# Sixty-four gate groups on the matrix engine: one fp32 product a token in place of three bfloat16 parts

## The reference

```python
def block(hb):
    q = (hb @ w_pq).reshape(TOK_BLOCK, PEER_HEADS, 2, PEER_DHALF)
    s = jnp.einsum('thpd,hpnd->thpn', q, sub_keys)
    s1, i1 = lax.top_k(s[:, :, 0], PEER_TOPK)          # first key, 16 of 128
    s2, i2 = lax.top_k(s[:, :, 1], PEER_TOPK)          # second key, 16 of 128
    cand_s = s1[..., :, None] + s2[..., None, :]
    cand_i = i1[..., :, None] * N_KEYS + i2[..., None, :]
    top_s, pos = lax.top_k(cand_s.reshape(..., 256), PEER_TOPK)
    idx = take_along_axis(cand_i, pos)                 # 16 experts a head, 8 heads
    gate = softmax(top_s)
    act = gelu(einsum('thkd,td->thk', expert_u[idx], hb))
    return einsum('thk,thkd->td', gate * act, expert_v[idx])
```

## Time and profile before

| | |
|---|---|
| median of three runs | 1565.65 us |
| profiled execution | 1565.16 us, span 1563.0 us |
| TensorE busy | 1477.0 us (94%) |
| VectorE busy | 1063.6 us (68%) |
| ScalarE busy | 724.0 us (46%) |
| GpSimd busy | 306.3 us (20%) |
| from the first to the last group of gates | 916.05 to 1144.1 us |
| gate products (x768) on TensorE | 55.8 us busy |
| one-hots (`EB`, x128) on VectorE | 48.4 us busy |
| one-hots times gate (`Ao`, x128) on VectorE | 65.4 us busy |

### The profile page before, as it was taken

How to read it: one execution, slowest core, us unless ns; L and a number is a source line. 1 busy time by engine, 2 the same in 40 slices (tenths; PEclk the granted TensorE clock), 3 DMA queues, 4 the chain that set the end, 5 groups by cost and what they waited for, 6 DMA issues and landing times.

```text
span 1563.0 us, 24880 instructions
## 1 busy us (share of the span) xinstructions
PE 1477.0 (94%) x10282; PEld 1323.2 (85%) x10282; DVE 1063.6 (68%) x1814; ACT 724.0 (46%) x1193; POOL 306.3 (20%) x143
## 2 busy tenths in 40 slices
PE   7999899999989778889999999999999999999998
PEld 6887687998877667878999999999998888888886
DVE  5665555665467988453599988999965555555554
ACT  4574444554344434214444454444444444444443
POOL 0046000000045420237799900000000000000000
PEclk9999999999999878779999999999999999999999
DMA  7623433555553300024565554444455666666663
GB/s 272 214 85 133 160 108 114 183 182 196 188 151 104 117 28 2 23 68 136 169 187 174 164 162 150 148 148 143 146 172 162 188 189 188 188 189 189 189 188 121
DMA packets 64879, 235.25 MB, mean 151 GB/s; under 512 B 7424, under 2 KB 7680, under 8 KB 64512
## 3 DMA queue, kind: packets, MB, share of 16 engines
q1 hardware_dynamic: 63904, 231.60, 46.9%
q10 hardware_dynamic: 864, 2.08, 0.4%
HBM read 232.60 MB, written 1.05 MB: 149 GB/s over the span
## 4 chain that ended last, share of the span: by engine, by line
PE 81%; DVE 10%; POOL 3%; ACT 3%; issue 1%; DMA 1%; ACTq 0%; DVEq 0%
PE ps L130 79%; POOL spl L145 3%; PE ps L139 1%; ACT spl L142 1%; DVE spl L145 1%; DVE prep L145 1%; DVE pR L145 1%; DVE pm L145 1%; DMA raw<-in_w_in_a 1%; DVE be L145 1%; DVE pm L154 1%; ACT QK L142 1%; DVE hx L145 1%; DVE junk L145 1%; DMA par<-in_par 0%
## 5 line engine op out<-in xcount | busy, mean ns | idle before, releaser
L130 PE MATMUL ps<-xhl,spl 128*128 128x256 f32 x4944 | 608.5, 283 | 11.3 <-POOL spl L145 9.6
L130 PEld LDWEIGHTS ps<-xhl,spl 128*128 128x128 f32 x4944 | 592.7, 189 | 14.9 <-POOL spl L145 11.2
L142 ACT ACTIVATE spl<-raw 128x1024 fp32r<-128x1024 f32 (+1 forms) x435 | 454.3, 1048 | 320.0 <-PE ps L130 302.0
L145 DVE TENSOR_TENSOR spl<-raw,spl 128x1024 fp32r<-128x1024 f32 (+1 forms) x329 | 402.6, 1229 | 222.7 <-ACT spl L142 220.9
L130 PE MATMUL ps<-spl,Wr 128*128 128x512 f32 x1536 | 358.6, 396 | 3.3 <-DVE Wr L145 3.3
L130 PEld LDWEIGHTS ps<-spl,Wr 128*128 128x128 f32 x1536 | 290.4, 189 | 71.3 <-DVE Wr L145 3.6
L145 POOL TENSOR_TENSOR spl<-raw,spl 128x1024 fp32r<-128x1024 f32 (+1 forms) x106 | 274.4, 2606 | 283.9 <-ACT spl L142 283.4
L142 ACT ACTIVATE Wr<-GE 128x256 fp32r<-128x256 f32 x128 | 53.3, 417 | 183.5 <-PE ps L130 183.5
L142 ACT ACTIVATE GE<-ps 128x256 f32<-128x256 f32 (+42 forms) x176 | 56.9, 326 | 126.6 <-DVE GE L145 109.9
L145 DVE TENSOR_TENSOR Wr<-GE,Wr 128x256 fp32r<-128x256 f32 x128 | 54.4, 426 | 81.2 <-ACT Wr L142 81.2
L130 PE MATMUL ps<-spl,ahl 128*128 128x512 f32 x384 | 90.1, 397 | 0.0
(11 more groups left out here) (337 smaller groups left out, 1236.4 us busy)
## 6 DMA issues: line engine op xcount, KB each, us to landing
raw<-in_eu SPq DMA_DIRECT2D x128, 512.0 KB, 3.6
raw<-in_ev SPq DMA_DIRECT2D x128, 512.0 KB, 4.0
raw<-in_w_up SPq DMA_DIRECT2D x32, 512.0 KB, 3.6
raw<-in_w_down SPq DMA_DIRECT2D x32, 512.0 KB, 4.2
raw<-in_w_in_a SPq DMA_DIRECT2D x16, 512.0 KB, 5.2
raw<-in_w_pq SPq DMA_DIRECT2D x16, 512.0 KB, 3.5
raw<-in_w_rwkv SPq DMA_DIRECT2D x14, 512.0 KB, 3.7
raw<-in_w_in_t SPq DMA_DIRECT2D x8, 512.0 KB, 3.5
```

Of the source, the lines that this page charges most:

```text
L130: return Done(self, self.e and self.e.matmul(out, l, r, start=st, stop=sp))
L142: return Done(self, self.e and self.e.activation(out, a, f, bias=bias, scale=scale, accum_out=acc))
L145: return Done(self, self.e and self.e.tensor_tensor(out, a, b, op))
```

## The change

The gates are no longer parted. `Ao` holds fp32 gates at their one-hot places, `EB` the fp32 one-hot of the second key alone, and a token's gates come from one fp32 product.

```diff
-        gp = SE("gp", [128, 3, 256], BF16)
-        EB = SE("EB", [128, 2, 2, 2, 128, 2], BF16)
+        EB = SE("EB", [128, 2, 4, 128])
-        Ao = SO("Ao", [128, 2, 3, 2, 128, 2], BF16)
-        io2 = SO("io2", [128, 128, 2], BF16)
-        idx = SO("idx", [128, 2, 256], BF16)
+        Ao = SO("Ao", [128, 2, 4, 128])
+        idx = SO("idx", [128, 2, 256])
...
                 for q in range(4):
-                    for k in range(3):
-                        last = pe.mm(b[:, q * 128:q * 128 + 128], EB[:, g % 2, 1, q // 2, :, q % 2], Ao[:, g % 2, k, q // 2, :, q % 2], k == 0, k == 2)
+                    last = pe.mm(b[:, q * 128:q * 128 + 128], EB[:, g % 2, q, :], Ao[:, g % 2, q, :], True, True)
...
-            def parted():
-
-                dve.wait_ge("slT")
-                for k in range(3):
-                    v = dve.cp(gp[:, k, :], sg[:, :]).own()
-                    dve.after(v)
-                    if k < 2:
-                        dve.after(dve.tt(sg[:, :], sg[:, :], gp[:, k, :], ALU.subtract).own())
-                return v
...
-                ts = slice(4 * g, 4 * g + 4)
-                eb, ao = EB[:, g % 2, :, :, :, :], Ao[:, g % 2, :, :, :, :]
-                pair = lambda t, a: bc(t[:, :, 4 * g + 2 * a:4 * g + 2 * a + 2], 2, 128)
-                made = [dve.tt(eb[:, :, a, :, :], bc(io2[:, :, :], 1, 2), pair(idx, a), ALU.is_equal).own() for a in range(2)]
-                for a in range(2):
-                    dve.after(made[a])
-                    x = dve.tt(ao[:, :, a, :, :], bc(eb[:, 0, a, :, :], 1, 3), pair(gp, a), ALU.mult)
+                dve.tt(EB[:, g % 2, :, :], bc(C("iota"), 1, 4), bc(idx[:, 1, 4 * g:4 * g + 4], 2, 128), ALU.is_equal)
+                for q in range(4):
+                    t = slice(4 * g + q, 4 * g + q + 1)
+                    x = dve.ts(Ao[:, g % 2, q, :], C("iota"), idx[:, 0, t], sg[:, t], ALU.is_equal, ALU.mult)
...
-            dve.wait_ge("h4")
-            dve.cp(io2[:, :, :], bc(C("iota"), 2, 2)).own()
...
-                    dve.after(parted())
+                    dve.wait_ge("slT")
```

More of the change, by code:

```diff
@@ L2416, in choose @@
                 dve.wait_ge("sel_ps", tb)
+                dve.wait_ge("h4")
                 ts = slice(tb * 128, tb * 128 + 128)
```

## The result

The changed kernel takes 1571.7 us (median of 9 runs, 1567.91 to 1572.87) against 1565.65 us before (9 runs). The ratio is 1.0038 with a 95% interval of 1.0027 to 1.0049, so it is slower by 0.4%, 4.2 to 7.7 us. I had forecast 1573.0 us, 7.3 us slower; the true loss is small but real. The profiled execution took 1572.19 us with a span of 1570.0, 7.0 us above that of before.

The account below looks back on a forecast made before the run. TensorE was taken to bound the kernel; +8.3 us for the gate groups, -1.0 at the start and 0 for other edits made +7.3, so a median of 1573.0 us, with eight in ten between 1567 and 1579.

Parts of the forecast that it names:

- What bounds: In the gates' stage TensorE sets the pace, with a level period of 3.607 us a group before the change.
- The group gets 0.13 us longer: On TensorE, four fp32 products replace twelve bfloat16 ones: 0.68 us to the next product becomes 0.81, 64 times, +8.3 us.
- by passes alone: Gate products on TensorE counted as four passes a token replacing three, all at 0.057 us: +14.6 us.
- the fp32 products' full 0.892 us: Upper bound for TensorE's gate group: old end loss stays, fp32 products add their full time, 0.21 us a group, +13.6 us.
- The start: Ahead of the first gate group, without the five parting instructions TensorE's wait for VectorE goes: -1.0 us.
- VectorE hides: In the gates' stage VectorE's five instructions take 1.41 to 1.65 us against 1.61, its chunk staying under TensorE's 3.74.
- rival 2: VectorE becomes the bound late in the gates' stage, tensor_scalar starts over 0.28 us apart: 1575 to 1580 us, chance 0.09.
- Rival 1: The fp32 gate group loses at its border as the old one did: +12.6 us, 1578.3, chance 0.10.
- Rival 3: A gate product of 128 columns is cheaper than in the key scores: -15 us, 1550.5, chance 0.03.
- Rival 4: TensorE's waits during the choice shift, up to three of about 1.1 us go: +4.0 us, 1569.7, chance 0.06.
- the signs: Expected in the trace after: 512 fp32 gate records, 57 us busy, groups 3.74 us apart, no wait before the first group.

Follow-up runs that it names:

- fp32_5: The changed kernel with the first token's fp32 product issued twice, five products a group instead of four: 1587.15 us, 1.0138 of the kernel before.
- bf16_16: The kernel before with the first part's product of each token issued twice, 16 bfloat16 products a group instead of 12: 1579.8 us, ratio 1.0092.
- eb_twice: The changed kernel with VectorE building the second key's one-hot twice a group: 1592.85 us, 1.0171 of the kernel before.

## Why the prediction was right

**What bounds.** TensorE sets the pace: a product more costs its own time and 64 times that in the median (`fp32_5`, `bf16_16`), and the period was level. Shown.

**The group gets 0.13 us longer.** Measured 3.733 - 3.607 = 0.126 us, 64 x 0.126 = 8.1 us against +8.3. The group to its successor is 0.81 us, as worked out from the key scores. The choice that mattered was which way to count: by passes alone this term would have been 14.6 us, 6 too many, and with the fp32 products' full 0.892 us on top of the old border's loss 13.6 us, 5 too many. The slopes confirm why: four short products and an fp32 product cost the same inside a group, and the group of short ones costs 0.065 to 0.09 us beyond its products, the fp32 group nothing. The prediction had the reason too: both kinds of group cost the scores behind them 0.08 us, and the early start behind a long fp32 record gives it back. The measured 2.92 to 2.93 us for the scores behind either kind bears that out. The Trainium skill's page "FP8 and Floating Point Precision", section "TensorE Precision Notes", with its four passes agrees with 0.227 against 4 x 0.056; it doesn't speak of the border. What makes the scores behind a group 0.08 us late was not settled. Their weights take 0.19 us to load, more than a short product's turn of 0.058 us, but the loss is as large behind fp32 records, whose turns are twice as long, so that alone does not explain it.

**The start.** -1.0 us forecast; TensorE's wait of 0.99 us is gone, and it came back as 1.01 with the parting. Shown.

**VectorE hides.** Right, but its price was at the far end of what I gave: a tensor_scalar with two numbers from memory is 0.344 us, the upper bound, and starts are 0.255 apart. The five instructions take 1.63 us where the four took 1.61. Operations with scalars saved VectorE nothing. The comparison and the second number did not cost the form its rate, the question that no row had answered: 0.344 us is the 0.284 us with one number plus 0.060 for one more, and at the pace of a tensor_tensor it would have been 0.064 longer. `eb_twice` puts the room left at 0.13 us a chunk, so rival 2 was 0.1 us away: it needed starts over 0.28 apart.

**The rivals.** Rival 1 is out: the period is 3.73 us and not 3.82. The scores behind the group do lose their 0.08 us, and the group gains it at its last record. Rival 3 is out: the records take 0.112 us. Rival 4 is out: the six waits for GpSimd during the choice are 6.5 us in all, 6.4 before.

**What it had wrong.** Among the signs, it gave the gate products 57 us of busy time, which is 512 turns of 0.112 us; the page counts to the end of each group's last record, and they are 67.4 us, some 1.05 for each of 64 groups. It also said that ScalarE waits until TensorE has used a piece. In the gates' stage of the kernel before, ScalarE waited for that once, 1.5 us, and it waited 108.1 us for VectorE's products (`GE`). Neither enters the sum.

**The size.** The median moved by 6.1 us where the trace has 7.0 and the forecast said 7.3; the interval, 4.2 to 7.7, holds all three. The forecast called a loss of this size one that may or may not be seen; with nine runs of each kernel it is seen, with an interval clear of no change. That the median came within 1.3 us of the forecast is partly luck, as the runs of one kernel spread over 5 to 6 us; the trace's +7.0, term by term, is the better witness.

## What to carry to other kernels

Where TensorE sets the pace, count its time by what stands in the trace, group to group, and not by instructions: four products in place of twelve were 0.13 us longer. An exact fp32 product of a one-hot and a number costs what four short ones cost, so splitting the number pays as long as there are fewer than four parts. Two fp16 parts gave 16 us here, at the price of the gate's lowest bits, whose effect on the result no run here measured. Before moving products together, see which buffer the second one needs: the border saved 0.09 us a pair, and the wait for a PSUM bank cost up to 0.41. And read a wait from the period rather than from the idle time listed, where records overlap the next start.

## What the hardware showed that I had not expected

- A tensor_scalar of 128 fp32 elements costs 0.284 us with one number from memory and 0.344 with two; at 256 elements it is 0.288 with none and 0.348 with one, so each such number adds 0.060 us.
- Score products behind a group of other products lose 0.08 us, be the group of short or of fp32 products; the next product starts 0.03 us after the group's last record, however long that record's turn is.
- Products of 128 columns in fp16 run at the pace of bfloat16: 0.219 us median in both, and 8 of them fit the line of 12 and 16.
- The stage with `ev`, the same program in all executions, took 362.9 to 366.0 us in ten profiled executions, a spread of half the loss that was to be measured.
